# Row gathers of a mixture-of-experts layer that pass over the unused slots of expert tiles

## The chip, the cores and the metric

One core of one Trainium2 chip runs the whole program. The metric is the time of one execution on the device, in microseconds (us). The profile is of one further execution; its instruction times come from the hardware profiler.

## The reference

A backbone of two layers over 256 context tokens and 256 latent tokens of width 1024. Layer 0 mixes with a recurrent and a convolution group, layer 1 with attention for the latent tokens alone. After the mixer each layer has a grouped mixture of experts: 16 experts, of which each token uses 2. Layer 0 sends 512 tokens through it, layer 1 sends 256.

```python
def grouped_moe(h, router_w, router_bias, w_gate, w_up, w_down):
    scores = jax.nn.sigmoid((h @ router_w).astype(jnp.float32))
    sel = scores + router_bias.astype(jnp.float32)
    grp_score = lax.top_k(sel.reshape(-1, N_GROUPS, EXPERTS_PER_GROUP), 2)[0].sum(-1)
    best = jnp.argmax(grp_score, axis=-1)
    in_group = (jnp.arange(N_EXPERTS) // EXPERTS_PER_GROUP)[None, :] == best[:, None]
    _, idx = lax.top_k(jnp.where(in_group, sel, -jnp.inf), TOP_K)
    w = jnp.take_along_axis(scores, idx, axis=-1)
    w = w / jnp.sum(w, axis=-1, keepdims=True)
    gates = jnp.sum(jax.nn.one_hot(idx, N_EXPERTS, dtype=jnp.float32) * w[..., None], axis=1)
    out = jnp.zeros_like(h)
    for e in range(N_EXPERTS):
        y = (jax.nn.silu(h @ w_gate[e]) * (h @ w_up[e])) @ w_down[e]
        out = out + gates[:, e:e + 1].astype(h.dtype) * y
    return out
```

Each of the three weights of an expert is 2 MiB in float32, so the experts of one layer are 96 MiB. The kernel reads all of them, whatever the router chose.

## The kernel before

**Tiles.** The kernel computes each expert only for the tokens that chose it. The tokens of an expert are put into tiles of 32 slots (`MT`). Expert after expert gets as many tiles as it needs, so the last tile of each expert has unused slots at its end. A token row of 1024 values is cut into four quarters, and a tile lies in SBUF as 128 partitions: partition 32q + s holds quarter q of slot s, 256 values or 1 KiB.

**The index table.** `route(l)` (VectorE) finds for every token its expert, its tile and its slot. Two one-hot matrices, `oh_slot` (which slot) and `oh_tile` (which tile, times the token's number), are multiplied on TensorE. For a used slot the product holds four times the token's number inside its block of 128 tokens in one column group, and the number of the block in the other. For an unused slot it holds zero in both. L1330 and L1331 make from these the row number `gidx` = 4 x 128 x block + 4 x token + quarter, where the quarter comes from `pcol[:, 2]`. So an unused slot gets the rows 0 to 3 of the table `h_rows`: it is filled with a copy of token 0, whose product is later not used (its gate value is zero, and in layer 0 no token reads that row of `y_rows`).

**The gathers.** GpSimd (POOL) issues one indirect DMA for each tile, from `h_rows` in HBM into one of four buffers `xg_in` (`gather(u, at)` in `moe(l)`, L1962; the first of a layer goes straight to `xg`, L1971). Five tiles are fetched before the loop, and the loop fetches tile k + 5 while tile k is computed. It fetches in rounds of four tiles and doesn't stop at the last tile, so the last five gathers of a layer are of tiles in which no slot is used. The list of other work on POOL in one trip: copy the landed tile to `xg` (L1966), copy the index column (L1997), issue the gather, and then, in layer 0, store the finished tile to `y_rows` (L2009), in layer 1 copy the tile's column of `slot_tab` (L2005).

**The compute.** VectorE transposes `xg` (L1210), TensorE multiplies by the expert's gate and up weights (L775), ScalarE and VectorE make the activation (L1757, L1373, L1375), TensorE multiplies by the down weight (L785), VectorE scales (L1397 or L1392). In layer 0 all tiles go to `y_rows` in HBM, and after the last one each token fetches its two rows (L2035). In layer 1 a matrix product (L752) adds them up on the chip.

**The weights.** SyncE issues the weight loads in a fixed order, gate, up and down of each expert, into three sets of three slots. Before it issues a load it waits until the slot's last user is done (`expert_done`) and until the load before the last has landed (the wait on `landed[before]` in `load_expert`), so at most two weight loads are under way:

```python
for m in range(3):
    free(m)
    if trio is not None:
        sp.sem_inc(s_par, 1)
        before = (3 * b + m - 2) % (3 * SETS)
        sp.wait_ge(landed[before], trio * 16 + 16 * (ahead[l][before] + (before < 3 * b + m)))
    load(l, e, b, m)
```

A load lands when all 16 DMA engines have added 1 to its semaphore.

Of the kernel before, what the change touches and what calls it, by code (L numbers as in the profile page):

```python
# [17 lines left out]
ALU = mybir.AluOpType  # L18
# [3 lines left out]
P = 128  # L22
# [4 lines left out]
NT = TOK // P  # L27
CT = CTX // P
# [15 lines left out]
AHEAD = 4  # L44
GMAX = MAXTILES + 2 * AHEAD + 1
MAXT = TOK // MT


C_C, C_CC, C_MIXG, C_CONVB, C_CONVW = 0, 8, 16, 32, 36
# [50 lines left out]
def build(nc, a):  # L100
# [9 lines left out]
    with ExitStack() as ctx:  # L110
# [11 lines left out]
        ps = ctx.enter_context(nc.psum_tensor("ps", [P, 8, 512], F32))  # L122
# [11 lines left out]
        iota_g = sb("iota_g", [P, GMAX])  # L134
        thr = sb("thr", [P, MAXT - 1])
        tile_no = sb("tile_no", [P, 2, NT])
        tie = sb("tie", [P, 4, 4])
        pcol = sb("pcol", [P, 4])
# [35 lines left out]
        u = reg(2048, 2048).rearrange("p (j n) -> p j n", j=JT)  # L174
# [28 lines left out]
        gidx = reg(12288, GMAX).bitcast(I32)  # L203
        slot_tab = reg(12288 + GMAX, 2 * GMAX).rearrange("p (g c) -> p g c", c=2)
        xg, xgT = reg(0, 256), reg(256, 256)
        act_sl, act_in, actT = reg(512, 128), reg(640, 128), reg(768, 128)
        xg_in = [reg(1024 + 256 * i, 256) for i in range(AHEAD)]
# [52 lines left out]
        s_xgs = [sem(f"tile_rows_gathered{u}") for u in range(AHEAD)]  # L260
# [675 lines left out]
        def _(dve):  # L936
            v = nc.vector
# [274 lines left out]
            def route(l):  # L1212
                tiles = toks(l)
                n = len(tiles)
                w = E * n
                at = [(1160, 1388)[l]]
# [53 lines left out]
                dve.wait_ge(s_pos, l + 1)  # L1270
                cmp_, ntile, incl, base = large(E * (MAXT - 1)), tmp(E), tmp(E), tmp(E)
                c3 = cmp_.rearrange("p (e m) -> p e m", e=E)
# [60 lines left out]
                if l:  # L1333
                    link(v.tensor_scalar(slot_tab[:, :, 0], ids, 0.25, pcol[:, 3:4], ALU.mult, ALU.subtract))
                    link(v.scalar_tensor_tensor(slot_tab[:, :, 0], ps[:, 4, 0:GMAX], 0.25, slot_tab[:, :, 0], ALU.mult, ALU.add))
                    link(v.tensor_copy(slot_tab[:, :, 1], ps[:, 4, 2 * GMAX:3 * GMAX]))
                    read_columns(1)
                    link(add_bias(1, 10, 12))
                    dve.sem_inc(s_mods, 1)
                else:  # L1340
                    v.tensor_scalar(slot_tab[:, :, 0], ps[:, 4, GMAX:2 * GMAX], CT - 0.5, None, ALU.is_lt)
                    read_columns(1)
                    choice_gates()
                    for c in range(2):
                        link(v.tensor_tensor(oh_gate[:, n * c:n * c + n, :], i3[:, n * c:n * c + n, :],
                                             gates2[:, c, 0:n].unsqueeze(2).to_broadcast([P, n, GMAX]), ALU.mult))
# [509 lines left out]
        def _(pool):  # L1856
            g = nc.gpsimd
            step = [0]

            def link(ins):  # L1860
                step[0] += 1
                ins.then_inc(s_pool, 1)
                pool.wait_ge(s_pool, step[0])
# [20 lines left out]
            kw = dict(allow_small_or_imprecise_dtypes=True)  # L1884
            link(g.iota(iota_s[:, :], [[0, 4], [1, MT]], base=0, channel_multiplier=0, **kw))
            link(g.iota(iota_g[:, :], [[MT, GMAX]], base=0, channel_multiplier=0, **kw))
            link(g.iota(thr[:, :], [[MT, MAXT - 1]], base=MT, channel_multiplier=0, **kw))
            link(g.iota(tile_no[:, :, :], [[0, 2], [1, NT]], base=0, channel_multiplier=0, **kw))
            link(g.iota(pcol[:, 0:1], [[0, 1]], base=0, channel_multiplier=1, **kw))
            link(g.iota(tie[:, :, :], [[1, 4], [-1, 4]], base=0, channel_multiplier=0, **kw))  # L1890
            link(g.tensor_scalar(tie[:, :, :], tie[:, :, :], 0.0, None, ALU.is_gt))
# [2 lines left out]
            for row in (64.0, 96.0):  # L1894
                link(g.tensor_scalar(pcol[:, 3:4], pcol[:, 0:1], row, None, ALU.is_ge))
                link(g.tensor_tensor(pcol[:, 2:3], pcol[:, 2:3], pcol[:, 3:4], ALU.add))
            link(g.tensor_scalar(pcol[:, 3:4], pcol[:, 2:3], 0.25, None, ALU.mult))
            pool.sem_inc(s_const, 1)


# [13 lines left out]
            for i in range(3):  # L1914
                rows = y_dram[E * MT + TOK * i:min(E * MT + TOK * i + TOK, (MAXTILES + AHEAD) * MT), :]
# [26 lines left out]
            def moe(l, before=None):  # L1942
                tiles = toks(l)
                n = len(tiles)
                for i, t in enumerate(tiles):
                    pool.wait_ge(s_h[l], 2 * i + 2)
                    g.dma_start(h_dram[l][P * i:P * i + P, :], hrow[:, t - CT * l, :]).then_inc(s_hst[l], 16)
                if not l:
                    pool.wait_ge(s_mrow, 2)
                    g.dma_start(mod_dram[0][:, 3].rearrange("v (k n) -> k v n", n=P),  # L1950
                                mod_rows[1].rearrange("p (v n) -> p v n", v=2)).then_inc(s_mst, 16)
                    pool.wait_ge(s_mst, 64)
                    for dst, c in ((g2_diff, CON), (g2_lat, LAT)):
                        quarter_rows(dst, mod_dram[0][c, 3])
                pool.wait_ge(s_rt[l], 1)
                pool.wait_ge(s_hst[l], 16 * n)
                rows = h_dram[l].rearrange("t (q n) -> (t q) n", q=4)
                places = y_dram.rearrange("(g s) (q n) -> g q s n", s=MT, q=4)

                def gather(u, at):  # L1960

                    g.indirect_dma_start(xg_in[u], None, rows, bass.IndirectOffsetOnAxis(at, 0)).then_inc(s_xgs[u], 16)  # L1962

                def bring(u):

                    g.tensor_copy(xg, xg_in[u]).then_inc(s_xg[l], 1)  # L1966

                def gathered(u, count):
                    return (count if before is None else before + (count + (0 if u else 1) + 1)) * 16

                g.indirect_dma_start(xg, None, rows, bass.IndirectOffsetOnAxis(gidx[:, 0:1], 0)).then_inc(s_xgs[0], 16)  # L1971
                for u in range(1, AHEAD):
                    gather(u, gidx[:, u:u + 1])
                total = pool.value_load(ctl[0:1, 2, E - 1:E], min_val=E, max_val=MAXTILES)
                if l:
                    pool.wait_ge(s_mrow, 4)
                    g.dma_start(mod_dram[1][3].rearrange("(k n) -> k n", n=P), mod_rows[3]).then_inc(s_mst, 16)
                pool.wait_ge(s_xgs[0], gathered(0, 1))
                pool.sem_inc(s_xg[l], 1)  # L1979
                gather(0, gidx[:, AHEAD:AHEAD + 1])  # L1980
                if l:
                    pool.wait_ge(s_mst, 128)
                    pool.wait_ge(s_rp[l], 2)
                    quarter_rows(g2_mat, mod_dram[1][3])
                    pool.wait_ge(s_gt[1], 1)
                    g.dma_start(fing, a["final_norm_g"].unsqueeze(0).to_broadcast([P, D])).then_inc(s_aux, 16)

                def four_tiles(j):

                    for u in range(AHEAD):  # L1990
                        k, nxt = j * AHEAD + u, (u + 1) % AHEAD
                        trips = 1 if nxt else 2
                        pool.wait_ge(s_xgs[nxt], gathered(nxt, j + trips))
                        pool.wait_ge(s_xgT[l], k + 1)
                        pool.sem_inc(s_pool, 1)
                        bring(nxt)
                        g.tensor_copy(gcur[:, nxt:nxt + 1], gidx[:, bass.ds(k + (AHEAD + 1), 1)]).then_inc(s_gc[l], 1)  # L1997
                        pool.wait_ge(s_xg[l], k + 2)
                        pool.wait_ge(s_gc[l], k + 1)
                        pool.sem_inc(s_pool, 1)  # L2000
                        gather(nxt, gcur[:, nxt:nxt + 1])
                        if l:
                            pool.wait_ge(s_spr, k + 1)
                            pool.sem_inc(s_pool, 1)
                            g.tensor_copy(slot_cur[:, :], slot_tab[:, k, :]).then_inc(s_cur, 1)  # L2005
                        else:
                            pool.wait_ge(s_y[0], k + 2)
                            pool.sem_inc(s_pool, 1)
                            g.dma_start(places[k], y_sb[u]).then_inc(s_yo[u], 16)  # L2009
                            if not isinstance(j, int) or nxt == 0:  # L2010
                                pool.wait_ge(s_yo[nxt], (j + (trips - 1)) * 16)
                                pool.sem_inc(s_yfree, 1)

                four_tiles(0)
                with pool.Fori(1, (total + (AHEAD - 1)) >> 2) as j:
                    four_tiles(j)
                rounds = (total + (AHEAD - 1)) >> 2
                if not l:
                    expert_rows(total)
                for u in range(AHEAD):  # L2020
                    pool.wait_ge(s_xgs[u], gathered(u, rounds + (1 if u else 2)))
                    if not l:
                        pool.wait_ge(s_yo[u], rounds * 16)
                pool.sem_inc(s_pool, 1)
                return rounds
# [65 lines left out]
```

## Time and profile before

| what | value |
|---|---|
| time, median of 3 runs | 963.18 us (962.91 to 963.35) |
| time of the profiled execution | 966.61 us |
| its span in the profile | 962.6 us |
| TensorE busy (matmul) | 806.8 us, 84% |
| VectorE busy | 450.0 us, 47% |
| GpSimd busy | 188.3 us, 20% |
| HBM read, written | 297.38 MB, 14.20 MB |

The profiled execution is 3.4 us longer than the median, and its span is 4.0 us shorter than its own time: what lies before the first and after the last instruction isn't in the span. Busy shares are means over the whole span. Layer 0's experts run from about 284 to 535 us, and layer 1's from about 730 to 952 us; between them lies the attention layer.

### The profile page before, as it was taken

Reading aid. Unit: us, or ns where it says so; the run is one execution under the profiler, and the core shown is the slowest. Engines: PE = TensorE matmul, PEld = TensorE weight load, DVE = VectorE, ACT = ScalarE, POOL = GpSimd, SP = SyncE. Lnnn points to the kernel's source line nnn. Section 1 sums busy time; section 2 is a strip of 40 time slices with the busy share of each in tenths; the row PEclk is TensorE's granted clock in tenths of the full one; section 3 lists DMA queues with packets and bytes.
Section 4 is the critical chain, followed back from the end, with each engine's and each line's share of the span. In section 5 each row is a group of like instructions: output and inputs, shape, how many; then the busy total and the mean of one; then the engine's idle time right before and its main releaser. Section 6 shows DMA issues by size and latency. Waiting matters only on the chain.

```text
span 962.6 us, 31597 instructions
## 1 busy us (share of the span) xinstructions
PE 806.8 (84%) x13340; PEld 538.5 (56%) x13341; DVE 450.0 (47%) x1101; ACT 265.1 (28%) x464; POOL 188.3 (20%) x364
## 2 busy tenths in 40 slices
PE   3899999899969898989888549999968885586985
PEld 2444444444457676778666435458436764464763
DVE  2379999943574343444433261765263221121222
ACT  2313436331413231322222130255032220121222
POOL 2300000010043332343323400000005220111220
PEclk9999999999979998999999969999998997788998
DMA  9992397578479999999999992881666999999992
GB/s 347 352 383 97 141 378 291 176 261 305 166 310 378 407 407 410 412 413 413 414 418 406 388 343 85 303 324 51 262 257 243 416 407 424 422 427 420 426 419 80
DMA packets 70692, 312.42 MB, mean 325 GB/s; under 512 B 8972, under 2 KB 9376, under 8 KB 54256
## 3 DMA queue, kind: packets, MB, share of 16 engines
q1 hardware_dynamic: 54608, 275.78, 72.6%
q0 software_dynamic: 15040, 33.62, 9.5%
q10 hardware_dynamic: 992, 2.26, 0.6%
q8 instruction: 40, 0.66, 0.3%
q14 instruction: 12, 0.10, 0.0%
HBM read 297.38 MB, written 14.20 MB: 324 GB/s over the span
## 4 chain that ended last, share of the span: by engine, by line
DMA 51%; PE 25%; DVE 18%; issue 3%; SPq 2%; ACT 2%; POOL 0%; DVEq 0%; POOLq 0%; ACTq 0%
DMA weight_ring<-in_exp_w_down 11%; DMA weight_ring<-in_exp_w_up 10%; DMA weight_ring<-in_exp_w_gate 10%; DVE arena L1068 9%; PE ps L608 7%; DMA arena<-in_exp_w_up 7%; DMA hT<-in_exp_w_down 5%; DMA arena<-in_exp_w_gate 4%; PE ps L831 3%; PE ps L874 3%; DMA weight_ring<-in_ev_w_in 2%; PE ps L574 2%; SPq L370 2%; PE ps L914 1%; PE ps L775 1%
## 5 line engine op out<-in xcount | busy, mean ns | idle before, releaser
L775 PE MATMUL ps<-weight_ring,arena 128*32 128x128 f32 x5760 | 183.0, 290 | 45.5 <-DMA weight_ring<-in_exp_w_up 27.9
L775 PEld LDWEIGHTS ps<-weight_ring,arena 128*32 128x32 f32 x5760 | 173.4, 118 | 60.0 <-issue 27.1
L1373 DVE TENSOR_TENSOR arena<-arena,ps 128x64 f32<-128x64 f32 x128 | 28.3, 221 | 225.9 <-ACT arena L1757 222.8
L1757 ACT ACTIVATE arena<-ps 128x64 f32<-128x64 f32 x128 | 28.7, 224 | 364.6 <-PE ps L775 364.6
L574 PE MATMUL ps<-hT,weight_ring 128*128 128x512 f32 x256 | 114.7, 604 | 2.8 <-DMA weight_ring<-in_ev_w_in 2.5
L785 PE MATMUL ps<-weight_ring,arena 128*32 128x256 f32 x1440 | 92.4, 382 | 6.6 <-DMA weight_ring<-in_exp_w_down 4.2
L1068 DVE SCALAR_TENSOR_TENSOR arena<-arena,par 128x512 f32<-128x512 f32 x132 | 94.9, 750 | 4.0 <-DVE arena L1099 0.8
L775 PE MATMUL ps<-arena 128*32 128x128 f32 x2432 | 74.3, 281 | 19.0 <-DMA arena<-in_exp_w_up 17.0
L574 PEld LDWEIGHTS ps<-hT,weight_ring 128*128 128x128 f32 x256 | 48.2, 192 | 67.3 <-issue 63.1
L775 PEld LDWEIGHTS ps<-arena 128*32 128x32 f32 x2432 | 70.8, 114 | 24.2 <-issue 22.6
L1757 ACT ACT_TABLE_LOAD x64 | 82.1, 1283 | 6.6 <-DVEq L1332 1.5
L1962 POOL DMA_INDIRECT arena<-h_rows,gcur x64 | 63.3, 989 | 50.5 <-POOL gcur L1997 48.9
L508 PE MATMUL ps<-weight_ring,cond 128*32 128x128 f32 x1536 | 54.5, 302 | 21.6 <-DMA weight_ring<-in_ada_w 21.0
L608 PE MATMUL ps<-weight_ring,arena 128*128 128x512 f32 x160 | 70.7, 596 | 1.0 <-DVE arena L1530 0.5
L785 PEld LDWEIGHTS ps<-weight_ring,arena 128*32 128x32 f32 x1440 | 42.0, 109 | 44.4 <-DVE arena L1375 21.2
L508 PEld LDWEIGHTS ps<-weight_ring,cond 128*32 128x32 f32 x1536 | 46.4, 121 | 33.9 <-DMA weight_ring<-in_ada_w 22.5
L2009 POOL DMA_DIRECT2D y_rows<-arena x40 | 30.5, 763 | 133.0 <-DVE arena L1397 114.8
L1966 POOL COPY arena<-arena 128x256 f32<-128x256 f32 x64 | 26.2, 409 | 148.9 <-issue 115.8
L608 PEld LDWEIGHTS ps<-weight_ring,arena 128*128 128x128 f32 x160 | 29.8, 190 | 37.8 <-issue 37.1
L785 PE MATMUL ps<-hT,arena 128*32 128x256 f32 x608 | 41.7, 398 | 4.1 <-DMA hT<-in_exp_w_down 3.2
L1210 DVE STREAM_TRANSPOSE arena<-arena 128x256 f32<-128x256 f32 x66 | 40.0, 605 | 3.7 <-POOLq L1979 2.1
L1397 DVE SCALAR_TENSOR_TENSOR arena<-ps,slot_cur,arena 128x256 f32 x40 | 19.4, 484 | 45.7 <-PE ps L785 45.7
(323 smaller groups left out, 868.9 us busy)
## 6 DMA issues: line engine op xcount, KB each, us to landing
weight_ring<-in_ada_w SPq DMA_DIRECT2D x24, 2048.0 KB, 14.2
weight_ring<-in_exp_w_gate SPq DMA_DIRECT2D x22, 2048.0 KB, 10.4
weight_ring<-in_exp_w_up SPq DMA_DIRECT2D x22, 2048.0 KB, 10.8
weight_ring<-in_exp_w_down SPq DMA_DIRECT2D x22, 2048.0 KB, 11.1
arena<-in_exp_w_gate SPq DMA_DIRECT2D x10, 2048.0 KB
hT<-in_exp_w_down SPq DMA_DIRECT2D x10, 2048.0 KB, 11.1
arena<-in_exp_w_up SPq DMA_DIRECT2D x10, 2048.0 KB
weight_ring<-in_ev_w_in SPq DMA_DIRECT2D x4, 2048.0 KB, 19.9
```

The source lines that it names most:

```text
L508: last = mm(ps[32 * g:32 * g + 32, bank, 0:P].rearrange("p (b i) -> p b i", b=4), cond[:, k, :], columns[:, g], start=(k == 0), stop=(k == ...
L574: last = mm(ps[:, m % 4, :], wide(slot)[:, k, P * j:P * j + P], hT[:, k, :], start=(k == 0), stop=(k == KD - 1))
L608: last = mm(ps[:, m % 4, :], lhs(k, i), wide(slot)[:, k, :], start=(k == 0), stop=(k == KD - 1))
L775: last = mm(ps[32 * qd:32 * qd + 32, 1 + hh, 0:P].rearrange("p (m n) -> p m n", m=2), xgT[:, MT * k:MT * k + MT], w2[:, k, :, at:at + 64], ...
L785: last = mm(ps[32 * qd:32 * qd + 32, down_bank, 0:256], actT[:, MT * step:MT * step + MT], wd[:, step, 256 * qd:256 * qd + 256], start=(st ...
L831: last = mm(ps[:, t, :], hT[:, k, P * t:P * t + P], wide(slot)[:, k, :], start=(k == 0), stop=(k == KD - 1))
L874: last = mm(ps[:, 4 + un, :], hT[:, k, P * (CT + i):P * (CT + i) + P], wide(slot)[:, k, :], start=(k == 0), stop=(k == KD - 1), skip_group ...
L1068: return v.scalar_tensor_tensor(o, src[:, j, :, w:w + CTX], wc, o, ALU.mult, ALU.add)
L1210: v.transpose(xgT.rearrange("p (k s) -> p k s", k=KD), xg.rearrange("p (i k) -> p k i", k=KD)).then_inc(s_xgT[l], 1)
L1757: s.activation(act_sl[:, 64 * hh:64 * hh + 64], ps[:, 1 + hh, 0:64], ACT.Silu).then_inc(s_sl[l], 1)
L1962: g.indirect_dma_start(xg_in[u], None, rows, bass.IndirectOffsetOnAxis(at, 0)).then_inc(s_xgs[u], 16)
L2009: g.dma_start(places[k], y_sb[u]).then_inc(s_yo[u], 16)
```

## The change

A used slot must keep its row number, and an unused slot must get one that lies beyond the table. The block numbers in `tile_no` now start at -64 (`NOWHERE`), and `pcol[:, 2]` is raised by 4 x 128 x 64 = 32768. In the sum these cancel for a used slot. For an unused one only the 32768 is left. The table has 2048 rows in layer 0 and 1024 in layer 1. Each gather of a tile gets `bounds_check` (the last row of the table) and `oob_is_err=False`: a row number above the bound is passed over, so that partition keeps what the tile before it in this buffer left there. `slot_tab` uses the same numbers, so its two formulas are corrected: the comparison in L1341 by 64, and `pcol[:, 3]` by 128 x 64. One more small operation on `pcol` is issued while the constants are made. The number of gathers, their order, and the stores of finished tiles stay.

```diff
+NOWHERE = 64
...
-                    v.tensor_scalar(slot_tab[:, :, 0], ps[:, 4, GMAX:2 * GMAX], CT - 0.5, None, ALU.is_lt)
+                    v.tensor_scalar(slot_tab[:, :, 0], ps[:, 4, GMAX:2 * GMAX], CT - 0.5 - NOWHERE, None, ALU.is_lt)
...
-            link(g.iota(tile_no[:, :, :], [[0, 2], [1, NT]], base=0, channel_multiplier=0, **kw))
+            link(g.iota(tile_no[:, :, :], [[0, 2], [1, NT]], base=-NOWHERE, channel_multiplier=0, **kw))
...
-            link(g.tensor_scalar(pcol[:, 3:4], pcol[:, 2:3], 0.25, None, ALU.mult))
+            link(g.tensor_scalar(pcol[:, 2:3], pcol[:, 2:3], 4.0 * P * NOWHERE, None, ALU.add))
+            link(g.tensor_scalar(pcol[:, 3:4], pcol[:, 2:3], 0.25, -P * NOWHERE, ALU.mult, ALU.add))
...
+                used_only = dict(bounds_check=4 * P * n - 1, oob_is_err=False)
...
-                    g.indirect_dma_start(xg_in[u], None, rows, bass.IndirectOffsetOnAxis(at, 0)).then_inc(s_xgs[u], 16)
+                    g.indirect_dma_start(xg_in[u], None, rows, bass.IndirectOffsetOnAxis(at, 0), **used_only).then_inc(s_xgs[u], 16)
...
-                g.indirect_dma_start(xg, None, rows, bass.IndirectOffsetOnAxis(gidx[:, 0:1], 0)).then_inc(s_xgs[0], 16)
+                g.indirect_dma_start(xg, None, rows, bass.IndirectOffsetOnAxis(gidx[:, 0:1], 0), **used_only).then_inc(s_xgs[0], 16)
```

## Rows read from the trace of the kernel before

**Rows 1.** The page's 40 slices (24 us each): DMA busy tenths, and GB/s

```profile
DMA  9992397578479999999999992881666999999992
GB/s 347 352 383 97 141 378 291 176 261 305 166 310 378 407 407 410 412 413 413 414 418 406 388 343 85 303 324 51 262 257 243 416 407 424 422 427 420 426 419 80
```

**Rows 2.** The page's chain that ended last: shares by engine, and by line

```profile
DMA 51%; PE 25%; DVE 18%; issue 3%; SPq 2%; ACT 2%; POOL 0%; DVEq 0%; POOLq 0%; ACTq 0%
DMA weight_ring<-in_exp_w_down 11%; DMA weight_ring<-in_exp_w_up 10%; DMA weight_ring<-in_exp_w_gate 10%; DVE arena L1068 9%; PE ps L608 7%; DMA arena<-in_exp_w_up 7%; DMA hT<-in_exp_w_down 5%; DMA arena<-in_exp_w_gate 4%; PE ps L831 3%; PE ps L874 3%; DMA weight_ring<-in_ev_w_in 2%; PE ps L574 2%; SPq L370 2%; PE ps L914 1%; PE ps L775 1%
```

**Rows 3.** The same chain in order of time, expert stages: start, us, what

```profile
284.06 22.77 DMA arena<-in_exp_w_up
...
514.86 11.18 DMA weight_ring<-in_exp_w_up
...
734.64 10.80 DMA weight_ring<-in_exp_w_gate
...
931.48 12.23 DMA weight_ring<-in_exp_w_down
```

**Rows 4.** Windows: us, busy of PE, PEld, DVE, ACT, POOL; PEclk, DMA share, GB/s

```profile
284.00:526.00 242.00, 216.34 (x6080) 174.60 (x6080) 99.71 (x306) 65.79 (x114) 89.16 (x155) 0.96 1.01 408
745.00:931.00 186.00, 141.66 (x3429) 112.54 (x3424) 42.11 (x136) 33.12 (x58) 32.85 (x78) 0.88 1.01 420
```

**Rows 5.** The page's packets and DMA queues (q1: SyncE's, q0: POOL's)

```profile
DMA packets 70692, 312.42 MB, mean 325 GB/s; under 512 B 8972, under 2 KB 9376, under 8 KB 54256
q1 hardware_dynamic: 54608, 275.78, 72.6%
q0 software_dynamic: 15040, 33.62, 9.5%
```

**Rows 6.** Groups of instructions by line, POOL: busy us, mean ns, idle before

```profile
L1962 POOL DMA_INDIRECT arena<-h_rows,gcur x64 | 63.3, 989 | 50.5 <-POOL gcur L1997 48.9 <-DVE arena L1210 0.8 <-DVE wbd L1388 0.8
L2009 POOL DMA_DIRECT2D y_rows<-arena x40 | 30.5, 763 | 133.0 <-DVE arena L1397 114.8 <-issue 15.9 <-DVEq L1402 2.3
...
L1962 POOL DMA_INDIRECT arena<-h_rows,arena x8 | 7.7, 961 | 2.4 <-issue 2.1 <-DMA arena<-h_rows,arena 0.3
...
L1906 POOL DMA_DIRECT2D wbd<-in_lru_w_r x4 | 2.7, 690 | 24.9 <-DVEq L1027 24.9
...
L1971 POOL DMA_INDIRECT arena<-h_rows,arena x2 | 2.1, 1037 | 17.4 <-DVEq L1332 17.4
...
L1897 POOL TENSOR_SCALAR pcol<-pcol 128x1 f32<-128x1 f32 x1 | 0.2, 218 | 0.1
```

**Rows 7.** Timeline of POOL, end of layer 0's experts: start, us, what

```profile
509.52 1.00 POOL L1962 DMA_INDIRECT arena<-h_rows,gcur  x1 [0.79 <-POOL gcur L1997]
512.88 0.76 POOL L2009 DMA_DIRECT2D y_rows<-arena  x1 [2.35 <-DVE arena L1397]
...
514.97 1.00 POOL L1962 DMA_INDIRECT arena<-h_rows,gcur  x1 [0.80 <-POOL gcur L1997]
...
538.05 1.00 POOL L1962 DMA_INDIRECT arena<-h_rows,gcur  x1 [0.79 <-POOL gcur L1997]
```

**Rows 8.** Landing times of the gathers issued by L1962, 500 to 545 us

```profile
DMA to landing us min/median/max: 5.9/8.8/10.6
```

**Rows 9.** Timeline of POOL, end of layer 1's experts

```profile
912.97 0.97 POOL L1962 DMA_INDIRECT arena<-h_rows,gcur  x1 [0.78 <-POOL gcur L1997]
...
934.92 0.97 POOL L1962 DMA_INDIRECT arena<-h_rows,gcur  x1 [0.78 <-POOL gcur L1997]
...
943.37 0.96 POOL L1962 DMA_INDIRECT arena<-h_rows,gcur  x1 [0.77 <-POOL gcur L1997]
```

**Rows 10.** Timeline of PE at the last expert of either layer

```profile
526.17 5.37 PE L775 MATMUL ps<-weight_ring,arena 128*32 128x128 f32 x128 [3.73 <-DMA weight_ring<-in_exp_w_up]
...
936.88 3.70 PE L775 MATMUL ps<-weight_ring,arena 128*32 128x128 f32 x128 [1.83 <-DMA weight_ring<-in_exp_w_up]
...
943.84 1.93 PE L785 MATMUL ps<-weight_ring,arena 128*32 128x256 f32 x32 [2.18 <-DMA weight_ring<-in_exp_w_down]
```

## The prediction, written before the change was timed

> **What bounds the kernel.** I read the chain that ended last first: 51% of it is DMA, and almost all of that is loads of expert weights [rows 2]. In order of time the chain goes through the whole of both expert stages from one weight load to the next, from 284 to 526 us in layer 0 and from 734 to 944 us in layer 1 [rows 3]. The slices say the same from another side: where the experts run, the DMA engines are busy in nine tenths or more and move over 400 GB/s [rows 1]. The windows are the decisive view: in the 242 us of layer 0's stage and in 186 us of layer 1's, the mean busy share of the 16 DMA engines is 1.01, so none of them ever idles; TensorE is busy 216.3 of 242 us and 141.7 of 186 us [rows 4]. So in these stages a byte less on a DMA engine is time won, as long as TensorE still has idle time to give up. At the last expert of layer 0 TensorE waits 3.73 us for the up weight, and at the last of layer 1 it waits 1.83 us for the up and 2.18 us for the down weight [rows 10]; each earlier wait moves with the loads too. TensorE therefore follows when the loads come some us earlier.
>
> **How many rows fall away.** There are 64 + 8 + 2 = 74 gathers [rows 6] of 128 rows of 1 KiB. Layer 0 stores 40 tiles [rows 6], so it has 1280 slots for 512 x 2 = 1024 tokens: 256 unused. It makes 40 + 5 = 45 gathers, the last five of empty tiles. Layer 1 has 74 - 45 = 29 gathers, so 24 tiles or 768 slots for 512 tokens: 256 unused again, and five empty tiles. Each layer thus fetches 256 + 5 x 32 = 416 slots for nothing, 1664 rows; both layers 3328 rows or 3.4 MB of 312 MB [rows 5].
>
> **What a row costs.** In layer 1's window 16 engines move 420 GB/s at a share of 1.01 [rows 4], so one moves 26.0 bytes a ns, and 1 KiB takes 39.4 ns. The other end is POOL's own queue: 9.5% of 16 x 962.6 us is 1463 us for 33.62 MB, or 44.6 ns for 1 KiB, small packets included [rows 5]. I take 42 ns.
>
> **How the saving is spread, and the sum.** A weight load lands when its slowest engine is done, and SyncE keeps at most two loads under way. An engine that saves much can run ahead of the slowest by less than a load; the stage then goes at the pace of the engine that saves least. Which rows of a gather an engine carries is not in the trace. But rows next to each other share an engine: if each of the 9472 gathered rows were a packet of its own, over 9472 packets would lie between 512 B and 2 KB, and there are 9376 - 8972 = 404 [rows 5]. Four rows to a packet would be 4 KiB. Unused slots are always the last of a tile, so an engine that carries the first slots saves little. I counted with the reference's router on its inputs: over the used tiles, groups of four slots (first to last) have 9, 24, 24, 29, 32, 33, 44 and 61 unused slots in layer 0, and 3, 13, 17, 26, 31, 46, 60 and 60 in layer 1; every empty tile adds 4 to each.
>
> Not every empty gather lies ahead of the weights that end the stage. In layer 0 the five are issued at 509.5, 515.0 and so on to 538.1 us [rows 7] and land 6 to 11 us later [rows 8]. The last load on the chain, the up weight, lands at 526.0 [rows 3], and TensorE needs the down weight 6 us after it. So two count for the one and at most four for the other: I count three. In layer 1 they are issued at 913.0 to 943.4, the fourth at 934.9 [rows 9], and the last load lands at 943.7 [rows 3]: four count.
>
> - Low end, 16 engines with 8 rows each, and one whose 8 rows are all of the first four slots. Layer 0: 9 + 3 x 4 = 21 slots, 2 rows each, 42 x 42 ns = 1.8 us. The two later empty gathers no longer stand before the last stores and the fetch from `y_rows`: at 8 rows x 42 ns each at most 0.7 us, of which I take 0.2. Layer 1: 3 + 4 x 4 = 19 slots, 38 x 42 ns = 1.6 us. Together 3.6 us.
> - High end, the saving even over the engines. Layer 0: 256 + 3 x 32 = 352 slots, 88 rows for each engine, 3.7 us; layer 1: 256 + 4 x 32 = 384, 96 rows, 4.0 us; with the 0.2, 7.9 us.
>
> I take 4.2 us. It lies near the low end since every load needs all engines, and a little above it since the engines need not be level when a stage begins: an engine that was ahead can stay behind the others' pace for some time before it sets the end. Both layers count in full: the tokens of layer 1 come from layer 0's sums, and what follows 526 us starts from there.
>
> The Trainium skill (DMA: Bandwidth & Descriptors, "The descriptor swizzle") says that for a transfer to 128 partitions engine 0 writes partitions 0 to 3 and 32 to 35, engine 8 writes 64 to 67 and 96 to 99, and so on; by it engines 0 and 8 carry just the first four slots, and the sum is the low end, 3.6 us. No run before the change shows it. The same page (section "Latency and other measured facts") calls engines 7 and 15 usually the slower ones; those would carry the last four slots, and were they the ones that set the pace now, the sum would be higher than the low end, up to what the next engines allow.
>
> **The other parts.** The extra operation on `pcol` takes 0.2 us, and POOL then waits 24.9 us for VectorE anyway [rows 6]; without that cover it would be 0.2 us. The new constants in `tile_no` and L1341 change no instruction's size: nothing. Gathers keep their count, and a gather lands 6 to 11 us after its issue with four tiles of lead, so a shorter landing helps nobody. No wait is added. What a bound check costs the gather instruction on POOL isn't in the trace. Below: nothing, or a little less than now, as fewer rows are written out. Above: I take the whole 1.0 us of the instruction again. In the densest part of layer 0 POOL's trip is 515.0 - 509.5 = 5.45 us, of which 2.35 us idle ahead of the store [rows 7]; so 1.0 us more is hidden, and I take 0.
>
> **Rivals.**
>
> *The saving counts evenly* (13%). It would need slack between the engines of several us over a stage, or rows dealt out so that each engine has early and late slots. For it: a stage begins and ends with unequal engines. Against it: adjacent rows go together. 963.2 - 7.9 = 955.3 us.
>
> *No traffic is saved* (16%). Passing over a row may mean a descriptor that still moves something or takes an engine as long. For it: nothing in the trace speaks of it, and packets of four rows look built ahead of any knowledge of the row numbers. Against: moving nothing is the plain reading of the operation. 963.2 us.
>
> *The check breaks up the packets* (slower, 13%). If each row becomes a packet, used rows cost more. POOL's queue took 1463 us; its bytes at 37.6 ns per 1000 would take 1264, which leaves 199 us over 15040 packets, 13 ns each [rows 5]. Four packets in place of one cost 3 x 13 / 4 = 10 ns more per used row. An engine of first slots has 45 x 8 - 58 = 302 used rows in layer 0 and 29 x 8 - 46 = 186 in layer 1: 488 x 10 ns = 4.9 us lost against 3.6 won, so 964.5 us. It ends slower from about 7.4 ns per used row up, where it takes all that was won; half the price is no change within the measurement.
>
> *POOL becomes the bound* (slower, 5%). The checked gather must take over 1.0 + 2.35 = 3.35 us before POOL holds up a tile in the densest part [rows 7]. At 5 us each, POOL's trip is 4 us longer, 5.45 - 2.35 + 4 = 7.1 us against 242 / 40 = 6.05 us for a tile: 40 x 1.05 = 42 us, 1005 us. Against it: nothing speaks for four times the work.
>
> **The numbers.** The forecast, pace of the engine that saves least, has 50%; its own range is 2.5 to 6 us won. The sum is made on the profiled execution (966.6 us, span 962.6); it is a difference, and I set it against the median of 963.18 us: 959.0 us, own range 957.2 to 960.7. The remaining 3% is for what I haven't thought of. For 8 times in 10 the range must hold the forecast, no saving, and part of the even case: 955.0 to 963.4. This kernel's measurement tells some 0.2%, 1.9 us, from no change. Faster: the forecast, nearly all (49%), the even case (13%) and a part of the broken packets and the unforeseen (6%): 68%. Same: no saving (16%) and some of the packets: 21%. Slower: 11%.
>
> **What would show it.** POOL's queue shows about 3.4 MB less, HBM reads too. The chain still goes from weight load to weight load in both stages; the pieces from 306 to 526 us and from 734 to 944 us are together some 2 us shorter in each layer, and the DMA share falls a little below 1.01, as the engines of late slots now wait. The gather instruction stays near 1 us. If the packets of POOL's queue under 2 KB number thousands more, they were broken up. If the bytes stay, nothing is passed over. The share staying at 1.01 with 4 us gone in each layer is the even case. The prediction is wrong above all if a passed-over row costs as much as a fetched one, or if the engines have more slack than I give them.

## The result

| kernel | runs | median | range |
|---|---|---|---|
| before | 6 | 963.04 us | 962.21 to 964.08 |
| changed | 6 | 956.83 us | 953.58 to 959.38 |

The ratio is 0.9926, with a 95% interval of 0.9909 to 0.9944: 5.4 to 8.8 us faster. Timed once more beside other kernels, the changed kernel had 956.63 us against 963.96 us, ratio 0.9910 (0.9892 to 0.9929). 959.0 us was forecast, 4.2 us won; measured are 6.2 and 7.3 us by the medians, 7.1 and 8.7 us by the ratios. The profiled execution took 957.07 us, with a span of 955.3 us.

The changed kernel's page first, in the lines that answer to [rows 1] and [rows 5]: slices, packets, POOL's queue, and HBM.

```profile
DMA  9992398568489999999999982881665999999992
GB/s 347 355 384 103 131 378 306 177 241 307 171 302 369 416 399 416 409 414 413 410 416 408 384 327 108 292 324 67 261 239 215 406 410 419 427 423 422 422 419 102
DMA packets 70694, 309.03 MB, mean 324 GB/s; under 512 B 9753, under 2 KB 10193, under 8 KB 54257
...
q1 hardware_dynamic: 54608, 275.78, 73.1%
q0 software_dynamic: 15040, 30.22, 8.8%
...
HBM read 297.38 MB, written 14.20 MB: 326 GB/s over the span
```

POOL's queue moves 33.62 - 30.22 = 3.40 MB less, which is 3328 rows of 1 KiB. It has the same 15040 packets as before. Some 781 of them are now under 512 B (9753 against 8972): a packet of which every row is passed over is still issued, but moves next to nothing, 16 bytes in the trace where a full one moves 4096. HBM read stands at 297.38 MB as before, though 3.40 MB less were read; this number doesn't follow the passed-over rows.

The chain in order of time, the pieces that answer to [rows 3] (start, us, what), and the windows that answer to [rows 4]. Layer 0's window ends 4 us earlier than before; layer 1's begins 3 and ends 5 us earlier:

```profile
512.31 10.01 DMA weight_ring<-in_exp_w_up
...
732.06 9.69 DMA weight_ring<-in_exp_w_gate
...
926.49 9.91 DMA weight_ring<-in_exp_w_down
```

```profile
core 0: us, PE busy (x) PEld busy (x) DVE busy (x) ACT busy (x) POOL busy (x), PEclk, DMA share, GB/s
284.00:522.00 238.00, 215.92 (x6080) 175.90 (x6072) 99.14 (x305) 65.80 (x114) 91.92 (x153) 0.97 1.01 408
742.00:926.00 184.00, 141.63 (x3410) 112.56 (x3406) 41.78 (x135) 33.11 (x58) 33.33 (x78) 0.89 1.01 419
```

The last binding load of layer 0 lands at 512.31 + 10.01 = 522.3 us, where it was 526.0: 3.7 us earlier. The last of layer 1 lands at 936.4 us, where it was 943.7: 3.6 us more. The rate is what it was, 408 and 419 GB/s (408 and 420 before). TensorE's matmuls in layer 0's window say nothing here: before, too, 6076 of the 6080 were done by 522 us, since it waited 3.73 us for the last up weight. In this pair of executions the time won in the two stages, 7.3 us, is about what the bytes that fell away are worth at the 39 ns a row found below.

The groups of POOL, which answer to [rows 6], and TensorE at the last experts, which answers to [rows 10]:

```profile
L1965 POOL DMA_INDIRECT arena<-h_rows,gcur x64 | 66.9, 1045 | 54.9 <-POOL gcur L2000 54.1 <-DVE arena L1211 0.9
L2012 POOL DMA_DIRECT2D y_rows<-arena x40 | 30.6, 764 | 123.3 <-DVE arena L1398 108.4 <-issue 12.6 <-DVEq L1403 2.3
```

```profile
522.45 5.08 PE L776 MATMUL ps<-weight_ring,arena 128*32 128x128 f32 x126 [2.56 <-DMA weight_ring<-in_exp_w_up]
...
931.58 3.70 PE L776 MATMUL ps<-weight_ring,arena 128*32 128x128 f32 x128 [1.51 <-DMA weight_ring<-in_exp_w_up]
...
936.53 1.93 PE L786 MATMUL ps<-weight_ring,arena 128*32 128x256 f32 x32 [0.17 <-DMA weight_ring<-in_exp_w_down]
```

A checked gather takes 1045 ns in place of 989. The 56 ns are hidden: POOL still waits 108.4 us for VectorE ahead of its stores. TensorE still waits for the weights at the last experts, 2.56 and 1.51 us for the up weights and 0.17 us for the last down weight, so it didn't become the bound.

### The profile page after: what moved, and what is told of

Its sections match the earlier page's. It is cut to its first block, busy times and chain, and to the rows that moved or that the text cites. A ratio compares the mean times of both kernels' runs of the same rounds, so it can differ in the third digit from the quotient of the medians.

```text
span 955.3 us, 31672 instructions
## 1 busy us (share of the span) xinstructions
PE 807.3 (85%) x13340; PEld 542.0 (57%) x13341; DVE 449.5 (47%) x1101; ACT 265.1 (28%) x464; POOL 193.3 (20%) x365
## 2 busy tenths in 40 slices
DMA packets 70694, 309.03 MB, mean 324 GB/s; under 512 B 9753, under 2 KB 10193, under 8 KB 54257
## 3 DMA queue, kind: packets, MB, share of 16 engines
q0 software_dynamic: 15040, 30.22, 8.8%
HBM read 297.38 MB, written 14.20 MB: 326 GB/s over the span
## 4 chain that ended last, share of the span: by engine, by line
DMA 50%; PE 25%; DVE 18%; issue 3%; SPq 2%; ACT 2%; POOL 0%; DVEq 0%; POOLq 0%; ACTq 0%
DMA weight_ring<-in_exp_w_down 10%; DMA weight_ring<-in_exp_w_up 10%; DMA weight_ring<-in_exp_w_gate 10%; DVE arena L1069 9%; PE ps L609 7%; DMA arena<-in_exp_w_up 7%; DMA hT<-in_exp_w_down 5%; DMA arena<-in_exp_w_gate 4%; PE ps L875 3%; PE ps L832 3%; DMA weight_ring<-in_ev_w_in 2%; PE ps L575 2%; SPq L371 2%; PE ps L776 2%; PE ps L915 1%
## 5 line engine op out<-in xcount | busy, mean ns | idle before, releaser
L776 PE MATMUL ps<-weight_ring,arena 128*32 128x128 f32 x5760 | 185.6, 292 | 45.9 <-DMA weight_ring<-in_exp_w_up 28.1
L776 PEld LDWEIGHTS ps<-weight_ring,arena 128*32 128x32 f32 x5760 | 175.8, 119 | 60.0 <-DMA weight_ring<-in_exp_w_up 26.8
L1965 POOL DMA_INDIRECT arena<-h_rows,gcur x64 | 66.9, 1045 | 54.9 <-POOL gcur L2000 54.1
L786 PEld LDWEIGHTS ps<-weight_ring,arena 128*32 128x32 f32 x1440 | 41.8, 109 | 39.4 <-DVE arena L1376 19.0
L2012 POOL DMA_DIRECT2D y_rows<-arena x40 | 30.6, 764 | 123.3 <-DVE arena L1398 108.4
## 6 DMA issues: line engine op xcount, KB each, us to landing
weight_ring<-in_exp_w_up SPq DMA_DIRECT2D x22, 2048.0 KB, 10.4
```

The source lines that it names most:

```text
L776: last = mm(ps[32 * qd:32 * qd + 32, 1 + hh, 0:P].rearrange("p (m n) -> p m n", m=2), xgT[:, MT * k:MT * k + MT], w2[:, k, :, at:at + 64], ...
L786: last = mm(ps[32 * qd:32 * qd + 32, down_bank, 0:256], actT[:, MT * step:MT * step + MT], wd[:, step, 256 * qd:256 * qd + 256], start=(st ...
```

## The experiments

Twelve kernels follow, in three groups; each group has its own timing of the kernel before. The question is where the 6 to 7 us come from: the forecast's pace of the engine that saves least gives 3.6 us, the bytes alone give 7.9.

**Is it the rows passed over, and is it the pace?** The first group has four kernels. All are the kernel before with the bound check on the gathers. In all four the expert rows of layer 0 are added with the factor 0, so that what a gather leaves out can't change layer 1's routing; they have 40 and 24 tiles, as the real kernel. Of the two additions and the two gather lines one each is printed; the others are changed likewise.

```diff
-                mark(v.tensor_tensor(x[:, i, :], x[:, i, :], yg[:, 1, i, :], ALU.add))
+                mark(v.scalar_tensor_tensor(x[:, i, :], yg[:, 1, i, :], 0.0, x[:, i, :], ALU.mult, ALU.add))
...
-                    g.indirect_dma_start(xg_in[u], None, rows, bass.IndirectOffsetOnAxis(at, 0)).then_inc(s_xgs[u], 16)
+                    g.indirect_dma_start(xg_in[u], None, rows, bass.IndirectOffsetOnAxis(at, 0), **used_only).then_inc(s_xgs[u], 16)
```

Three of them also raise the row numbers of some slots in every gather by 32768, over a mask made from the partition number (here slots 16 to 31; the others differ in the two divisors or the sign):

```diff
+            for col, k, w in ((4, 16.0, 1.0), (5, 32.0, -2.0)):
+                link(g.tensor_scalar(pcol[:, col:col + 1], pcol[:, 0:1], 1.0 / k, -(k - 1.0) / (2.0 * k), ALU.mult, ALU.add))
+                link(g.tensor_scalar(pcol[:, col:col + 1], pcol[:, col:col + 1], ROUND, None, ALU.add))
+                link(g.tensor_scalar(pcol[:, col:col + 1], pcol[:, col:col + 1], -ROUND, w, ALU.add, ALU.mult))
+            link(g.tensor_tensor(pcol[:, 4:5], pcol[:, 4:5], pcol[:, 5:6], ALU.add))
+            link(g.tensor_scalar(pcol[:, 4:5], pcol[:, 4:5], 32768.0, None, ALU.mult))
+            link(g.tensor_tensor(pcol[:, 2:3], pcol[:, 2:3], pcol[:, 4:5], ALU.add))
```

> The kernel before, with the bound check on every gather of a tile but row numbers that are never above the bound, so that nothing is passed over. It leaves one thing out, which keeps the routing of layer 1 the same in this run and the three beside it: the expert rows are added to x of layer 0 with the factor 0. All theories: POOL's gather takes 0.05 us more than the 0.99 us of before (as in the changed kernel), and that is hidden. 963 us, within 1.5 us of the kernel before. If the time falls by 5 us or more here, it was the checked form of the gather, not the rows passed over, that made the kernel faster.

> As the check-only kernel, but the rows of slots 16 to 31 of every tile get a number above the bound, so half of all gathered rows is passed over: 74 x 64 = 4736 rows. It leaves out the computation for these slots. A row costs about 35 ns of one engine by the change from before to after in POOL's queue (1463 to 1345 us for 3328 rows), so this is 4736 x 35 / 16 = 10.4 us of all engines. Theory A (a stage goes at the pace of the engine that saves least): the engines of slots 0 to 15 save nothing, so 0 to 2 us faster than the check-only kernel, and the DMA share in the stages falls by some 5 percent of a us for each us, to about 0.95 to 0.98. Theory B (every byte counts, whichever engine saves it): 9 to 11 us faster, share unchanged.

> The mirror of the kernel with the late slots passed over: here the rows of slots 0 to 15 of every tile are passed over, 4736 rows. It leaves out the computation for these slots. Theory A: 0 to 2 us faster than the check-only kernel. Theory B: 9 to 11 us. A third case: if only one of the two halves gives the time, the engines that carry that half are the ones that set the pace.

> Again 4736 rows are passed over, but those of the third and fourth slot of every four, so that each engine saves half of its rows. It leaves out the computation for these slots. Theory A and theory B alike: 9 to 11 us faster than the check-only kernel. The difference between this and the late-slots kernel is what an uneven saving costs: 8 to 10 us by theory A, none by theory B.

| kernel | median | ratio to before (966.77 us) | 95% interval |
|---|---|---|---|
| check only | 967.96 us | 1.0013 | 1.0002 to 1.0024 |
| slots 16 to 31 passed over | 965.62 us | 0.9992 | 0.9979 to 1.0006 |
| slots 0 to 15 passed over | 966.95 us | 1.0000 | 0.9986 to 1.0013 |
| two of every four passed over | 958.75 us | 0.9921 | 0.9903 to 0.9938 |

The check by itself gains nothing; the kernel with it is 1.2 us slower. The other addition isn't longer, 1220 ns in both traces, so what the 1.2 us are is not shown. The three that pass over rows pass over the same number, 4736, and POOL's queue shows 28.79 MB for each. Against the check-only kernel the spread one wins 9.2 us, the two one-sided ones 2.3 and 1.0 us. The late-slots kernel is a little above theory A's 0 to 2 us.

The packets show how the rows are grouped. These are the packet lines of the late-slots and the spread kernel:

```profile
DMA packets 70693, 307.60 MB, mean 319 GB/s; under 512 B 10156, under 2 KB 10560, under 8 KB 54256
```

```profile
DMA packets 70693, 307.60 MB, mean 322 GB/s; under 512 B 8972, under 2 KB 9376, under 8 KB 54256
```

With one half passed over (the early-slots page has the same numbers), 10156 - 8972 = 1184 = 74 x 16 packets more are under 512 B; with two of every four passed over, none. So a packet holds the rows of four neighbouring slots, as the prediction took it. The time that POOL's packets take, summed over the trace, falls from 1474.7 us in the check-only kernel to 1288.0, 1288.7 and 1288.0 us (late, early, spread): for the DMA engines taken together the three savings are the same. Only where they lie differs. So which rows fall away decides, and theory A holds for a saving this uneven: engines that save nothing set the pace. Which engine carries which packet is not in the trace. The windows of layer 0, 410 to 520 us: check only, slots 16 to 31 passed over, spread.

```profile
410.00:520.00 110.00, 96.73 (x2740) 78.38 (x2736) 44.98 (x137) 29.93 (x52) 41.85 (x69) 0.97 1.02 415
```

```profile
410.00:520.00 110.00, 96.57 (x2725) 78.73 (x2720) 44.74 (x136) 29.43 (x51) 40.74 (x68) 0.97 1.01 402
```

```profile
410.00:520.00 110.00, 99.01 (x2832) 80.27 (x2827) 47.00 (x143) 30.81 (x54) 43.05 (x72) 0.98 1.02 414
```

The last two columns are what to read. The rate falls from 415 to 402 GB/s where one half saves and stays at 414 where all save. The DMA share, which by my expectation was to fall to 0.95 to 0.98, stays at 1.01. It doesn't show engines that are ahead; the rate does. The single packets tell why: in this window the median 16 KiB weight packet takes 0.62 us in all three kernels. The longest takes 0.8 us (check only), 1.3 (spread) and 2.3 (late slots), and 0.6%, 0.8% and 6.1% of them take over 0.7 us. A packet that takes longer counts as busy all that time. That these are packets of the engines that are ahead is my reading.

**Which part of the change gives how much?** The second group: the changed kernel again, only the empty tiles, only the used ones, and another order of slots. For the two parts a mask of the tiles beyond the total is added to the row numbers (plus on the kernel before, minus on the changed one).

```diff
+                tot, far = tmp(1), tmp(GMAX)
+                link(v.tensor_scalar(tot, incl[:, E - 1:E], float(MT), -0.5, ALU.mult, ALU.add))
+                link(v.tensor_scalar(far, iota_g[:, :], tot, 32768.0, ALU.is_ge, ALU.mult))
+                link(v.tensor_scalar(far, far, pcol[:, 2:3], None, ALU.add))
                 dve.wait_ge(s_id, 1 + 2 * l)
...
-                link(v.tensor_scalar(ids, ps[:, 4, GMAX:2 * GMAX], 4.0 * P, pcol[:, 2:3], ALU.mult, ALU.add))
+                link(v.scalar_tensor_tensor(ids, ps[:, 4, GMAX:2 * GMAX], 4.0 * P, far, ALU.mult, ALU.add))
```

The other order, on the changed kernel:

```diff
-            link(g.iota(iota_s[:, :], [[0, 4], [1, MT]], base=0, channel_multiplier=0, **kw))
+            link(g.iota(iota_s[:, :], [[0, 4], [1, 8], [8, 4]], base=0, channel_multiplier=0, **kw))
...
-                    v.tensor_copy(row_i[:, :, 0:n], hl3)
...
+                    link(v.tensor_scalar(f8, s_, 1.0 / 8, -7.0 / 16, ALU.mult, ALU.add))
+                    link(v.tensor_scalar(f8, f8, ROUND, None, ALU.add))
+                    link(v.tensor_scalar(f8, f8, -ROUND, -31.0, ALU.add, ALU.mult))
+                    link(v.scalar_tensor_tensor(f8, s_, 3.0, f8, ALU.mult, ALU.add))
+                    link(v.tensor_tensor(row_i[:, :, 0:n], hl3, f8.rearrange("p (c t) -> p c t", c=2), ALU.add))
```

> The changed kernel, timed again beside the three others of this call: 5.5 to 7.5 us faster than before. All theories.

> Only the rows of the five empty tiles of each layer are passed over; the unused slots of used tiles fetch token 0 as before. These rows lie on all engines alike. 7 empty tiles lie ahead of the loads that end a stage: 896 rows x 37 ns / 16 engines = 2.1 us, and 0.2 us for what stood before the last stores. Strict pace of the engine that saves least, pace with slack, and every byte counts: all three 2.3 us faster than before (1.5 to 3).

> Only the unused slots of used tiles are passed over; the five empty tiles of each layer fetch token 0 as before. Strict pace: the engines of the first four slots save 9 + 3 slots x 2 rows x 37 ns = 0.9 us. Every byte counts: 512 slots x 4 rows x 37 ns / 16 = 4.7 us. Pace with slack (the half-kernels gained 1 to 2 us in two stages, so about 0.5 to 1 us a stage is given away by engines that are ahead): 2 to 3 us.

> The changed kernel, but the slots of a tile lie in another order on the partitions: slot s goes to place 4 x (s mod 8) + s div 8, so that neighbouring slots are on different engines and the unused ones fall on all engines nearly alike. The rows of y_rows follow (five small operations of VectorE more in layer 0's routing, beside a product of TensorE that takes 0.95 us, so up to 0.5 us lost). Every byte counts: as the changed kernel or 0.5 us slower. Strict pace: 736 slots x 4 rows x 37 ns / 16 = 6.8 us, plus 0.2, so 7.0 us faster than before and 3.5 us faster than the changed kernel. Pace with slack: 1 to 2 us faster than the changed kernel.

| kernel | median | ratio to before (963.96 us) | 95% interval |
|---|---|---|---|
| changed, again | 956.63 us | 0.9910 | 0.9892 to 0.9929 |
| empty tiles only | 961.95 us | 0.9978 | 0.9963 to 0.9993 |
| used tiles only | 960.08 us | 0.9956 | 0.9931 to 0.9981 |
| changed, interleaved slots | 956.25 us | 0.9921 | 0.9901 to 0.9942 |

The empty tiles give 2.0 us, as all theories said. The used tiles give 3.9 us where the strict pace allows 0.9, the pace with slack 2 to 3 and the bytes 4.7. The interval, 1.8 to 6.7 us, shuts out the strict pace by the first four slots, and neither of the other two. The interleaved order wins nothing measurable over the changed kernel, as the theory that every byte counts had it; the 3.5 us of the strict pace and the 1 to 2 us of the pace with slack didn't come. Page lines of POOL's queue, empty tiles only, then used tiles only:

```profile
q0 software_dynamic: 15040, 32.31, 9.3%
```

```profile
q0 software_dynamic: 15040, 31.53, 9.1%
```

They are 1.31 and 2.09 MB below the 33.62 of before, 1280 and 2048 rows: the count of the prediction.

**How can a very uneven saving be lost and a moderately uneven one not?** By the swizzle rule (the Trainium skill, DMA: Bandwidth & Descriptors, "The descriptor swizzle") each group of four slots has a pair of engines of its own; the one-sided kernels agree with it, as a half of the slots is clearly not carried by all engines. The third group of kernels: one group of slots alone is fetched, so that its engines save nothing and all others save everything.

```diff
+            for col, k, w in ((4, 4.0, 1.0), (5, 32.0, -8.0)):
...
+            link(g.tensor_scalar(pcol[:, 4:5], pcol[:, 4:5], -0.0, None, ALU.add))
+            link(g.tensor_tensor(pcol[:, 4:5], pcol[:, 4:5], pcol[:, 4:5], ALU.mult))
+            link(g.tensor_scalar(pcol[:, 4:5], pcol[:, 4:5], 0.5, None, ALU.is_ge))
+            link(g.tensor_scalar(pcol[:, 4:5], pcol[:, 4:5], 32768.0, None, ALU.mult))
+            link(g.tensor_tensor(pcol[:, 2:3], pcol[:, 2:3], pcol[:, 4:5], ALU.add))
```

(-0.0 is for group 0; -1.0, -4.0 and -7.0 for the others.)

> As the half kernels (bound check on, factor 0 on the expert rows of layer 0, so that layer 1's routing stays that of the check-only kernel), but every gather fetches slots 0 to 3 alone, and passes over the rows of the 28 others: 74 x 112 = 8288 rows. It leaves out the computation for these. By bytes 8288 x 37 ns / 16 = 19 us. One of the eight groups of four slots saves nothing. Theory N (the engines of the first slots are ahead of the others when nothing is passed over, by 2 us a stage or more, so the change's small saving there does not bind): 4 us or more faster than before. Theory S (all engines alike, and any of them can be behind by about 1 us a stage before it sets the pace): 1 to 2 us. Redistribution (an engine runs faster when the others have less to do, in proportion): 4 to 5 us here and in all four kernels of this call alike, as the late-slots kernel gained a fifth of its bytes.

> The same, with slots 4 to 7 fetched alone. It leaves out the computation for the 28 others. Theory N: the late-slots kernel gained 2.3 us against the check-only one with slots 0 to 15 fetched, so the slowest of its four groups has 1.2 us a stage; this group 2 to 4 us faster than before. Theory S: 1 to 2 us.

> The same, with slots 16 to 19 fetched alone. It leaves out the computation for the 28 others. The early-slots kernel gained 1.0 us with slots 16 to 31 fetched. Theory N: 1 to 3 us faster than before, less than for slots 0 to 3. Theory S: 1 to 2 us.

> The same, with slots 28 to 31 fetched alone, those of engines 7 and 15 by the Trainium skill (DMA: Bandwidth & Descriptors, The descriptor swizzle), which that page calls usually the slower ones. It leaves out the computation for the 28 others. Theory N: these set the pace before, so 0 to 1 us faster than before, and clearly less than for slots 0 to 3. Theory S: 1 to 2 us, as for slots 0 to 3.

| fetched alone | median | ratio to before (964.42 us) | 95% interval | won |
|---|---|---|---|---|
| slots 0 to 3 | 958.63 us | 0.9950 | 0.9932 to 0.9969 | 4.8 to 5.8 us |
| slots 4 to 7 | 962.85 us | 0.9987 | 0.9971 to 1.0002 | 1.3 to 1.6 us |
| slots 16 to 19 | 962.93 us | 0.9991 | 0.9974 to 1.0007 | 0.9 to 1.5 us |
| slots 28 to 31 | 960.38 us | 0.9950 | 0.9931 to 0.9968 | 4.0 to 4.8 us |

(The last column gives the two readings, by ratio and by medians. The check-only kernel, 1.2 us slower than before in the first group of kernels, wasn't timed here.) Each passes over 8288 rows, worth 19 us by the 37 ns a row of the expectation, and none wins more than 5.8. The group that isn't relieved sets the pace, and the groups aren't alike. I call what a kernel wins while one group keeps its full load that group's lead: the engines of slots 0 to 3 and of 28 to 31 can carry their full load and the kernel still gets 4 to 6 us faster, those of slots 4 to 7 and 16 to 19 only 1 to 1.5 us. So theory N holds for the first slots, misses its 2 to 4 us for slots 4 to 7, and fails for the last slots: I had expected those to be the slowest. The Trainium skill (DMA: Bandwidth & Descriptors, "Latency and other measured facts") calls engines 7 and 15 usually slower; if they are the ones of the last four slots, this case speaks against it. Redistribution in proportion would give all four kernels the same time; it falls. A smaller speed-up of the loaded engines, alike in all four, isn't excluded; it can't be more than the least gain here, 0.9 to 1.5 us by slots 16 to 19. Engines that carry eight neighbouring partitions each, in place of two times four, fall too: then every engine would save at least half its rows, as in the spread kernel, and each of the four would win at least the 8.0 us that the spread one won over the kernel before. The windows of layer 0 again, slots 0 to 3 alone and slots 28 to 31 alone:

```profile
410.00:520.00 110.00, 97.00 (x2722) 79.11 (x2716) 44.66 (x136) 29.34 (x51) 40.77 (x68) 0.95 1.00 392
```

```profile
410.00:520.00 110.00, 96.40 (x2676) 78.23 (x2670) 43.32 (x132) 29.21 (x50) 39.66 (x66) 0.95 1.00 389
```

At a share of 1.00 the engines move 392 and 389 GB/s, where they can move 415.

## Why the prediction was right, and by how much it was off

**The bound.** Right. The weight loads carry both stages before and after, and TensorE gave up waiting time only: it is busy 806.8 us before and 807.3 after. The step to it was weaker than it looked, though. A mean share of 1.01 was read as engines that never idle, and the kernel that fetches slots 0 to 3 alone has a share of 1.00 at 392 GB/s where 415 are possible.

**The count of rows.** Right: 3328, 3.40 MB less in POOL's queue.

**The price of a row.** 42 ns was a little high. By the page the queue's time fell from 9.5% of 16 x 962.6 us to 8.8% of 16 x 955.3 us, 1463 to 1345 us: 118 us over 3328 rows is 35 ns, but the rounding of the shares allows some 5 ns either way. The packet times summed over the traces are finer: 1470.6 to 1342.3 us, 39 ns a row. The three half kernels give 39 ns too, and the four with one group of slots fetched, against the check-only kernel, 39 to 42. I use 39 ns below; the 35 to 37 ns of the expectations came from the rounded shares.

**The spread over the engines.** This step was mis-sized, and it is the whole difference. The medians of the changed kernel, 956.83 and 956.63 us, lie just outside the forecast's own 957.2 to 960.7 us. They lie in the stated range because that was widened for the rivals, so that much of the hit is luck. The term "one engine whose 8 rows are all of the first four slots" (3.6 us) with 0.6 us on top for engines that aren't level was to give 4.2 us; the change won 6.2 and 7.3 us. The pace rule itself was shown: the same number of rows wins 9.2 us when spread and 1.0 to 2.3 when one-sided. What was wrong is which engines bind. The ones of the first four slots have a lead of 4.8 to 5.8 us over the two stages, not 0.6. Adding each group's saving (its slots of the prediction's count ahead of the last loads, 2 rows of 39 ns each, both layers) to the lead measured in the third group of kernels:

- slots 0 to 3: 40 slots, 3.1 us, lead 4.8 to 5.8: 7.9 to 8.9 us
- slots 4 to 7: 36 + 29 slots, 5.1 us, lead 1.3 to 1.6: 6.4 to 6.7 us
- slots 16 to 19: 44 + 47 slots, 7.1 us, lead 0.9 to 1.5: 8.0 to 8.6 us
- slots 28 to 31: 73 + 76 slots, 11.6 us, lead 4.0 to 4.8: 15.6 us or more

The least is 6.4 to 6.7 us, by slots 4 to 7, and 6.6 to 6.9 with the 0.2 us after the stage. For used tiles alone the same sum has 37 slots in that group, 2.9 us, so 4.2 to 4.5 us, and 3.9 us was measured (4.2 by the ratio). The intervals of the change, 5.4 to 8.8 and 6.8 to 10.4 us, hold 6.8 to 8.8 in common, and the sum reaches their lower end. The leads have an uncertainty of 1.5 us, and they may hold the common speed-up named above, which the change wouldn't have. Four of the eight groups were measured, and the sum joins separate runs; I call the pace rule and the unequal leads shown, and slots 4 to 7 as the ones that bind in the change a reading that fits.

**The rivals.** The even case, 7.9 us, is nearest to the profiled pair, 3.7 and 3.6 us in the stages at an unchanged rate, and its 955.3 us are nearer to 956.83 than the forecast's 959.0. The change alone doesn't tell it from unequal leads, since 7.4 us by bytes at 39 ns (736 slots of 4 rows over 16 engines, and 0.2) and 6.6 to 6.9 by groups hardly differ. Its reason, that it doesn't matter which engine saves, falls with the one-sided kernels. No traffic saved: the queue's bytes say no. Packets broken up: 15040 before and after. Its price was off besides: it stood on 37.6 ns per 1000 bytes, where the 26.0 bytes a ns of the prediction make 38.5, so 11 ns a packet in place of 13. POOL as the bound: 1045 ns a gather, far from the 3.35 us that it would take.

**What I said would show it.** The falling DMA share as a sign of engines that wait was wrong: it stays at 1.01 in the late-slots kernel, where the rate says that they do. So the sign named for the even case, the share at 1.01 with 4 us gone in each layer, came true here and tells nothing. HBM reads were to fall by 3.4 MB and didn't, though POOL's queue shows the rows gone.

**Still open.** Why the engines of the first and the last slots have a lead isn't shown; neither is why the interleaved order, with 7.4 us by bytes (7.6 and 7.7 measured) and a nearly even saving, isn't above the changed kernel by the 0.5 to 0.8 us that the group sum would leave it. That lies inside the intervals. And the spread kernel won 9.2 us where 4736 rows at 39 ns over 16 engines are 11.5: some part of an even saving is lost too, and no run shows where.

## What to carry to other kernels

When the DMA engines are the bound, small transfers beside the big ones cost their bytes, and rows that nobody uses are worth passing over: 3.4 of 312 MB gave 0.7% here. Ask which engines the saved rows lie on, since a big load waits for its last engine: a saving on half of the engines is mostly lost, one that is moderately uneven isn't. To tell which it is, pass over the same number of rows once spread and once on one side, and read GB/s, not the busy share.

## What the runs showed of the hardware

- A row that the bound check passes over keeps its place in a packet: 15040 packets before and after, 781 more of them under 512 B. It moves 4 bytes (a packet of four such rows has 16) and saves 39 ns of one engine for 1 KiB.
- The checked form of the gather takes 1045 ns on POOL for 128 rows against 989, whether no row, half or seven eighths are passed over (1045 to 1048 in all these kernels).
- A packet of these gathers holds the rows of four neighbouring partitions: 1184 = 74 x 16 packets shrink when half of the slots is passed over on one side, none when two of every four are.
- The DMA share of the profile stays at 1.00 to 1.02 while the rate falls from 415 to 389 GB/s where part of the engines have far less to move than the ones that set the pace. Some weight packets take longer instead, up to 2.6 us where the median is 0.61.
- The HBM read count of the page is the same, 297.38 MB, with and without the 3.4 MB.
- Engines aren't level: fetched alone, the rows of slots 0 to 3 or 28 to 31 leave 4 to 6 us of gain, those of slots 4 to 7 or 16 to 19 only 1 to 1.5 us.
